# First stage of a two-block transformer kernel: token scale moved into the band matrix, Pool products ordered by token tile, one stacked one-hot product

## The reference

```
def rmsnorm(x, g):
    y = xf * lax.rsqrt(jnp.mean(xf * xf, axis=-1, keepdims=True) + EPS)
    return (y * g.astype(jnp.float32)).astype(x.dtype)

def pool_mixer(h, w, scale):            # h = rmsnorm(x, norm_mixer[0]), T = 256, D = 1024
    for g, win in enumerate((2, 4, 8, 16)):        # four groups of 256 features
        window_sum = csum[:, 1:, sl] - jnp.take(csum[:, :, sl], start, axis=1)
        outs.append(window_sum / cnt[None, :, None] - hf[:, :, sl])
    d = jnp.stack(outs, axis=2).astype(h.dtype)
    y = jnp.einsum('btgc,gce->btge', d, w).reshape(B, T, D)
    return y * scale

x = x + pool_mixer(rmsnorm(x, norm_mixer[0]), pool_w[0], pool_scale[0])
x = x + swiglu(rmsnorm(x, norm_ffn[0]), w_gate_up[0], w_down[0])
```

## Time and profile before

| what | value |
|---|---|
| median of 3 runs | 1152.99 us (1152.88 to 1153.0) |
| the profiled execution's own time | 1156.47 us |
| its span | 1154.5 us |
| PE busy | 1130.8 us, 98% of the span |
| DVE, ACT busy | 778.4 us (67%), 536.0 us (46%) |
| DMA | 204.57 MB, mean 177 GB/s |

### The profile page before, as it was taken

One profiled execution on the slowest core, in us unless ns is written; L12 is line 12 of the kernel. 1 busy time (PEld: TensorE's weight loads), 2 busy tenths in 40 slices (PEclk: granted clock), 3 DMA queues, 4 the chain that ended last, 5 costly groups with the idle time before them and its releaser, 6 DMA issues. The chain is left out here.

```text
span 1154.5 us, 16968 instructions
## 1 busy us (share of the span) xinstructions
PE 1130.8 (98%) x6628; PEld 983.2 (85%) x6628; DVE 778.4 (67%) x998; ACT 536.0 (46%) x704; POOL 32.8 (3%) x47
## 2 busy tenths in 40 slices
PE   6999999999999999999999999999999999999997
PEld 6788888898888888879988888888899888888886
DVE  4866666856667666677576676666766766766665
ACT  4633333466654334444566443334446655343332
POOL 0000000000000000003000000000030000000000
PEclk9999999999999999999999999999999999999999
DMA  8665555673356555668423465556673234656550
GB/s 271 224 201 183 200 182 189 222 245 113 118 174 230 187 182 182 207 153 264 144 104 103 148 230 195 182 182 201 179 235 110 75 111 145 219 188 201 181 193 37
DMA packets 167131, 204.57 MB, mean 177 GB/s; under 512 B 19988, under 2 KB 150028, under 8 KB 167078
## 3 DMA queue, kind: packets, MB, share of 16 engines
q1 hardware_dynamic: 167078, 203.84, 55.1%
HBM read 202.66 MB, written 1.16 MB: 177 GB/s over the span
## 5 line engine op out<-in xcount | busy, mean ns | idle before, releaser
L633 ACT ACTIVATE whi<-raw 128x2048 fp32r<-128x2048 f32 x176 | 336.4, 1914 | 381.2 <-PE bank L1514 247.2
L948 DVE TENSOR_TENSOR wlo<-raw,whi 128x2048 fp32r<-128x2048 f32 x171 | 392.0, 2294 | 163.1 <-ACT whi L633 163.0
L1510 PE MATMUL bank<-h_both,whi 128*128 128x512 f32 x1280 | 304.6, 390 | 0.0
L1510 PEld LDWEIGHTS bank<-h_both,whi 128*128 128x128 f32 x1280 | 237.7, 188 | 47.7
L1484 PE MATMUL bank<-whi,o_hi 128*128 128x512 f32 x448 | 176.2, 393 | 0.0
L1485 PE MATMUL bank<-wlo,o_hi 128*128 128x512 f32 x448 | 174.9, 390 | 0.0
L1486 PE MATMUL bank<-whi,o_lo 128*128 128x512 f32 x448 | 174.4, 389 | 0.0
L1514 PEld LDWEIGHTS bank<-h_both,wlo 128*128 128x128 f32 x1280 | 164.1, 191 | 6.2
L1514 PE MATMUL bank<-h_both,wlo 128*128 128x256 f32 x1280 | 166.0, 283 | 0.0
L1486 PEld LDWEIGHTS bank<-whi,o_lo 128*128 128x128 f32 x448 | 84.1, 188 | 18.0
L1484 PEld LDWEIGHTS bank<-whi,o_hi 128*128 128x128 f32 x448 | 84.3, 188 | 17.7 <-issue 1.3
(11 more groups left out here) (176 smaller groups left out, 1181.0 us busy)
## 6 DMA issues: line engine op xcount, KB each, us to landing
raw<-in_w_gate_up SPq DMA_DIRECT2D x44, 1024.0 KB, 5.1
raw<-in_w_down SPq DMA_DIRECT2D x44, 1024.0 KB, 4.9
raw<-in_w_gate SPq DMA_DIRECT2D x22, 1024.0 KB, 5.3
raw<-in_w_up SPq DMA_DIRECT2D x22, 1024.0 KB, 5.3
raw<-in_w_in SPq DMA_DIRECT2D x20, 1024.0 KB, 5.9
raw<-in_w_o SPq DMA_DIRECT2D x12, 1024.0 KB, 5.0
raw<-in_w_kv SPq DMA_DIRECT2D x8, 1024.0 KB, 5.4
raw<-in_w_q SPq DMA_DIRECT2D x4, 1024.0 KB, 5.4
```

The costliest lines, as they stand in the source:

```text
L633: act.activation(whi[:, s, :], raw[:, s, :], ACT.Copy).then_inc(hi_ready, 1)
L948: dve.tensor_tensor(wlo[:, s, :], raw[:, s, :], whi[:, s, :].bitcast(F32), ALU.subtract).then_inc(lo_ready, 1)
L1510: pe.matmul(bank[bk + jj][:, :], hi[:, kc, jj * P:(jj + 1) * P], h_both[:, kc, :, :].rearrange("p a t -> p (a t)"), start=(kc == 0), stop= ...
```

## The change

- The gain is no longer replicated over all partitions: its 1024 numbers are loaded as 8 rows of 128, PE transposes them to 8 columns (L1659), ACT copies these to `gcol` (L763). They are applied as a per-partition scale when d is copied out of the banks: ACT and DVE now do so in 8 pieces of 256 columns each (L777, L1298), DVE with a `scalar_tensor_tensor`.
- x itself is the stationary operand of the band products. The token scale `rstd` goes into the band: one `tensor_scalar` of 128x640 for each token tile (`scaled_band`, L1274) in place of four `normalise` of 128x512. The band is stored once (160 instead of 272 columns for each group), partition-major.
- The fourth square goes to DVE (`tensor_tensor_reduce`, L1278).
- ACT and DVE split both halves of the Pool weights ahead of all copies of d.
- The Pool products run in the order (0,0), (0,1), (1,0), (1,1), into banks 4 to 7; `first_norm` is rewritten for that order.
- The two tables and the two one-hot matrices are stacked at partitions 0 and 64: one product (L1690, 97 rows, 24 columns of weights), one copy (L678). Their loads stand ahead of the first gate weights on SP, behind a wait for three memsets on DVE. The product waits for the third `pool_scale`, since it uses bank 6.
- The identity matrix is loaded as the third DMA.

```
-            load_gain(0)
-            sp.dma_start(band, c["c_band"].rearrange("g p n -> p g n")).then_inc(band_in, 16)
+            sp.dma_start(ident[:, :], c["c_ident"]).then_inc(ident_in, 16)
+            sp.dma_start(gain_rows, GAIN_SRC[0].rearrange("(k p) -> k p", p=P)).then_inc(gains_in[0], 16)
+            sp.dma_start(band, c["c_band"].rearrange("p g n -> p (g n)")).then_inc(band_in, 16)
...
+            sp.wait_ge(ones_set, 2)
+            sp.dma_start(tables[0:NBUCKET, 0:16], a["rel_bias"]).then_inc(table_in, 16)
+            sp.dma_start(tables[T5_ROW:T5_ROW + NBUCKET, 16:24], a["t5_table_2"]).then_inc(table_in, 16)
+            sp.dma_start(onehots, c["c_onehots"]).then_inc(onehot_in, 16)
             load(k8(ffn_weights(0)[0], 0), FFN_U[0])
-            sp.dma_start(ident[:, :], c["c_ident"]).then_inc(ident_in, 16)
...
-            for t in range(TT):
-                for h in range(2):
-                    square(0, t, h)
+            for t, h in ((0, 0), (0, 1), (1, 0)):
+                square(0, t, h, 2 if t else 1)
+            act.wait_ge(gain_turned, 1)
+            act.activation(gcol[:, :], bank[7][:, 0:KC], ACT.Copy).then_inc(gcol_ready, 1)
...
+            for part in range(2):
+                pool_whi(part)
+            act.wait_ge(gcol_ready, 1)
             for k in range(4):
-                if k % 2 == 0:
-                    pool_whi(k // 2)
                 act.wait_ge(pool_d, k + 1)
-                act.activation(h_hi[:, 2 * k:2 * k + 2, :], bank[k][:, :].rearrange("p (c k) -> p c k", c=2),
-                               ACT.Copy).then_inc(hT_hi, 1)
+                for c_ in (2 * k, 2 * k + 1):
+                    i = act.activation(h_hi[:, c_, :], bank[k][:, (c_ % 2) * T:(c_ % 2 + 1) * T], ACT.Copy, scale=gcol[:, c_:c_ + 1])
+                i.then_inc(hT_hi, 1)
...
                     pool_scale(0, 0)
-                    pool_scale(1, 0)
                     pool_add(0, 0)
                     pool_scale(0, 1)
                     pool_add(0, 1)
-                    pool_scale(1, 1)
+                    pool_scale(1, 0)
                     mean_square(1, 0)
                     normalise(1, 0, 0)
                     normalise(1, 0, 1)
                     pool_add(1, 0)
+                    pool_scale(1, 1)
+                    h_lo_out(1, 0, 0)
                     pool_add(1, 1)
-                    h_lo_out(1, 0, 0)
                     h_lo_out(1, 0, 1)
...
+            def scaled_band(t):
+
+                if t == 0:
+                    dve.wait_ge(band_in, 16)
+                dve.wait_ge(rstd_ready, t + 1)
+                dve.tensor_scalar(band_s[t], band, rstd[:, t:t + 1], None, ALU.mult).then_inc(xn_ready, 2)
 
             mean_square(0, 0)
-            normalise(0, 0, 0)
+            dve.wait_ge(x_in[1], 16)
+            dve.tensor_tensor_reduce(xn[:, 1, HALF:], x[:, 1, HALF:], x[:, 1, HALF:], 1.0 / D, 0.0, ALU.mult, ALU.add,
+                                     ssq[:, 1, 1:2]).then_inc(last_square, 1)
+            scaled_band(0)
+            dve.wait_ge(last_square, 1)
             mean_square(0, 1)
-            normalise(0, 0, 1)
-            for h in range(2):
-                normalise(0, 1, h)
+            scaled_band(1)
...
-            for h in range(2):
-                pe.wait_ge((pool_lo, lo_ready)[h], 1)
-                for t in range(TT):
+            for t in range(TT):
+                for h in range(2):
+                    pe.wait_ge((pool_lo, lo_ready)[h], 1)
...
+            pe.wait_ge(pool_out, 3)
+            pe.matmul(bank[6][0:24, :], tables[:, :], onehots, start=True, stop=True).then_inc(vec_done, 1)
```

More of the change, by code:

```diff
@@ L51 @@
 IN_W = 2720
-BAND_W = 2 * P + 16
+BAND_W = P + 32
+T5_ROW = 64
 POOL_U = 0
@@ L86, in shape_constants @@
     t = np.arange(T)
-    band = np.zeros((4, P, BAND_W), f)
+    band = np.zeros((P, 4, BAND_W), f)
     for g, win in enumerate((2, 4, 8, 16)):
@@ L234, in bass_two_stacks @@
         wukv = sb("wukv", [P, 4, 2, HD])
-        band = qall[:, :, :].rearrange("p k t -> p (k t)")[:, 0:4 * BAND_W].rearrange("p (g n) -> p g n", g=4)
-        onehots = bias[:, 0:2 * SEQ_D].rearrange("p (i n) -> p i n", i=2)
-        vecs = bias[:, 2 * SEQ_D:4 * SEQ_D].rearrange("p (i n) -> p i n", i=2)
+        band_flat = qall[:, :, :].rearrange("p k t -> p (k t)")
+        band = band_flat[:, 0:4 * BAND_W]
+        band_s = [band_flat[:, (1 + i) * 4 * BAND_W:(2 + i) * 4 * BAND_W] for i in range(TT)]
+        gain_rows = xn[0:KC, 0, 0:P]
+        onehots = bias[0:T5_ROW + NBUCKET + 1, 0:SEQ_D]
+        vecs = bias[:, SEQ_D:2 * SEQ_D]
         pool_y = pr[:, 0:4, :, :].rearrange("p i a b -> p i (a b)")
@@ L633, in split, with square @@
                     act.activation(whi[:, s, :], raw[:, s, :], ACT.Copy).then_inc(hi_ready, 1)
-            def square(version, t, h):
+            def square(version, t, h, count=1):
                 if version:
@@ L644, in square @@
                 act.activation(junk[:, :], x[:, t, h * HALF:(h + 1) * HALF], ACT.Square, scale=1.0 / 32,
-                               accum_out=ssq[:, t, h:h + 1]).then_inc(squares, 1)
+                               accum_out=ssq[:, t, h:h + 1]).then_inc(squares, count)
             def h_out(j, t, h):
@@ L1276, in pool_wlo @@
                                   ALU.subtract).then_inc((pool_lo, lo_ready)[part], 1)
+            for part in range(2):
+                pool_wlo(part)
+            dve.wait_ge(gcol_ready, 1)
             for k in range(4):
-                if k % 2 == 0:
-                    pool_wlo(k // 2)
                 dve.wait_ge(hT_hi, k + 1)
-                dve.tensor_tensor(h_lo[:, 2 * k:2 * k + 2, :], bank[k][:, :].rearrange("p (c k) -> p c k", c=2),
-                                  h_hi[:, 2 * k:2 * k + 2, :].bitcast(F32), ALU.subtract).then_inc(hT_lo, 1)
+                for c_ in (2 * k, 2 * k + 1):
+                    i = dve.scalar_tensor_tensor(out=h_lo[:, c_, :], in0=bank[k][:, (c_ % 2) * T:(c_ % 2 + 1) * T],
+                                                 scalar=gcol[:, c_:c_ + 1], in1=h_hi[:, c_, :].bitcast(F32),
+                                                 op0=ALU.mult, op1=ALU.subtract)
+                i.then_inc(hT_lo, 1)
             ffn(0)
@@ L1664, in _ @@
             used(mm)
-            pe.wait_ge(ones_set, 3)
+            pe.wait_ge(ones_set, 2)
             pe.wait_ge(table_in, 32)
-            pe.wait_ge(onehot_in, 32)
-            K = NBUCKET + 1
-            for i, lhs in enumerate((tab_moba[0:K, :], tab_t5[0:K, :])):
-                pe.matmul(bank[6 + i][0:lhs.shape[1], :], lhs, onehots[0:K, i, :], start=True, stop=True).then_inc(vec_done, 1)
+            pe.wait_ge(onehot_in, 16)
+            pe.wait_ge(pool_out, 3)
+            pe.matmul(bank[6][0:24, :], tables[:, :], onehots, start=True, stop=True).then_inc(vec_done, 1)
             def ffn(f):
```

63 lines of the change are left out of this document (29 added, 34 removed).

## The result

| | median (range, executions) |
|---|---|
| before | 1152.99 us (1151.73 to 1157.84, 20) |
| changed | 1154.76 us (1153.97 to 1155.65, 20) |

The account below looks back on a forecast made before the run. PE's work plus its idling bounds the kernel, early on via a DVE chain to tile 1's transposes. 1.8 + 1.42 - 0.1 - 0.65 = 2.5 us off 1152.99 gives 1150.5 us, range 1149.0 to 1152.7.

Parts of the forecast that it names:

- At nothing: Parts forecast to change no time: single one-hot product (saves about 0.9 us of PE, hidden), tables' loads, one ACT copy less.
- The tables' loads: they finish long before: Table and one-hot loads moved ahead of the gate weights: claimed to finish long before needed, so worth nothing.
- first band product earlier: Kernel start: band lands at 7.8, its scale takes 0.55, so PE starts at 8.4 instead of 10.20, 1.8 us earlier.
- from there to the first Pool product: Band products keep shapes and count, so still 10.6 us, from 8.4 to 19.0; no gain.
- new order, up to `normalise` of tile 0: Pool products: `normalise` needs two chunks, not three; 12 matmuls less save 1.42 us, minus 0.1 for DVE.
- scale (1,1) in DVE's chain: Between tile 0's `normalise` and tile 1's transposes: one more 128x512 DVE operation gives back 0.65 us.
- The power: POOL's power for tile 0's rstd, slowed beside DVE's square, ends at 7.6, before the band lands at 7.8.
- The one-hot product: Single product before tile 0's transposes: ends at 26.7 while xn comes at 27.1, so its saving is worth nothing.
- the copies in eight pieces: Copies of d after the band products: last low part at 21.0, wanted at 22.8, so hidden with 1.8 to spare.
- Rival 2: Clock rises early, at the second tile's band products: 3.7 us more, gain 6.2, 1146.8 us; chance 0.11.
- rival 4: Clock stays low through the first gate passes, which end 2.2 us later than before: 1155.3 us; chance 0.04.
- Rival 3: Front doesn't move, small transfers costing what the saved bytes gain: PE starts at 10.2, gain 0.7, 1152.3 us; chance 0.13.

Follow-up runs that it names:

- 128-row kernel: Changed kernel with the one-hot matrices stored and loaded as 128 rows instead of 97, the product still reading 97: 1150.62 us, ratio 0.9988 to before.
- 96 idle rows: Kernel before plus a load of 96 rows that nothing reads, ahead of the first gate weights: 1152.94 us, ratio 0.9999.
- 97 rows late: Changed kernel, 97-row one-hots kept, with tables and one-hots loaded in their old place behind the first up weights: 1154.99 us, ratio 1.0014 to before.
- second profile of before: Kernel before, unchanged, run and profiled again: 1152.62 us beside 1152.74, ratio 0.9999; profile span 1150.7 us.
- the square on ACT: Changed kernel with 128 stored one-hot rows and the fourth square back on ACT instead of DVE: 1150.37 us in one execution.
- two variants with the same front and order: Changed kernel with 128 one-hot rows: table and one-hot loads in their old place, 1150.47 us; or DVE's first-half up-weight split behind tile 1's `normalise`, 1150.69 us.
- 106 rows: Kernel before plus a load of 106 rows that nothing reads, ahead of the first gate weights: 1157.16 us, ratio 1.0039.
- 99 rows: Kernel before plus a load of 99 rows that nothing reads, ahead of the first gate weights: 1152.72 us, ratio 1.0.
- 97 idle rows: Kernel before plus a load of 97 rows that nothing reads, ahead of the first gate weights: 1161.05 us, ratio 1.0071.

## Why the prediction was wrong

**The step that failed** is, in "At nothing", "The tables' loads: they finish long before". I asked whether the moved loads are late for their own reader (they weren't: at 19.38 for a product at 22.88), and not what they do to the load behind them. The one-hots held one engine and with it 1/16 of the gate weights, which are waited for by ACT, behind which stand the squares. It cost 4.00 us at tile 1's transposes (33.97 against 29.97) and turned 2.1 us gained into 1.8 lost. The spans differ by more, 1153.5 against 1148.4: 1.2 us more is the fall of the clock at 523 us. The same matmuls are 3.97 us later in the changed kernel up to 522 us (the transposes just ahead: 521.24 and 517.27), and 5.20 us later from 528 us on. Where the 128-row kernel has sixteen matmuls 0.12 us apart, the changed one has them 0.21 apart:

```profile
523.08 0.42 PE L1558 MATMUL bank<-whi,h_both 128*128 128x256 f32 x1
523.30 0.42 PE L1559 MATMUL bank<-wlo,h_both 128*128 128x256 f32 x1
```

and the 128-row kernel:

```profile
519.02 0.28 PE L1559 MATMUL bank<-whi,h_both 128*128 128x256 f32 x1
519.14 0.28 PE L1560 MATMUL bank<-wlo,h_both 128*128 128x256 f32 x1
```

PE idled 1.35 us ahead of them, and 1.36 at the same place in the 128-row kernel, where nothing fell. Of the thirteen profiles of this case three more have a fall near there (522.3 us with 96 idle rows, 523.3 with 97, 516.6 with 97 rows late); why one falls and the other doesn't stays open. The fall at 28 us cost nothing: from `normalise` to the next transposes 7.17 us, against 7.15 at full clock, since DVE's chain sets that time.

**The other steps**, measured between the second profile of before and the 128-row kernel:

| term | predicted | measured |
|---|---|---|
| first band product earlier | 1.8 | 10.19 - 8.58 = 1.61 |
| from there to the first Pool product | 0 | 7.97 - 7.84 = 0.13 |
| new order, up to `normalise` of tile 0 | 1.42 - 0.1 = 1.32 | 7.75 - 6.40 = 1.35 |
| scale (1,1) in DVE's chain | -0.65 | 6.54 - 7.15 = -0.61 |
| sum | 2.5 | 2.48 |

Behind the first row: the band was there for its scale at 8.14 in the changed kernel, 7.97 with 128 rows and 7.81 with the square on ACT (forecast 7.8, bounds 7.2 and 8.3); the scale took 0.55 as estimated. The power ended at 7.4 (forecast 7.6) and is off the path: with the square on ACT it ended 0.5 earlier than in the 128-row kernel (6.69 against 7.20), and the chain from the band on was the same. The one-hot product, the gain's transpose and the copies in eight pieces were hidden as said.

**The clock.** Rival 2 had its place right: the rise falls among the second tile's band products, in the changed kernel and in each of its variants (the 48 products take 8.45 and 8.07 us in the two shown, 8.17 to 8.56 in the other five, where they took 11.01). In the trace its price is right too: 36.09 to 29.97 is 6.1 us, where I had worked out 6.2. But the kernel before gains by it as well: 36.09 to 32.45 in its two profiles, 3.6 us, where the rival had 3.7, and the execution with the early rise lies at the median (1152.76 beside 1152.62), the one with the late rise 3.5 above it. So it is no gain of the change. I had taken these 3.5 us as constant, and they weren't: the profiled execution lies 0.8 above the median in the changed kernel and 0.2 below it with 128 rows. That the forecast of 1150.5 fits the 128-row kernel all the same is in part luck: the sum compares two executions that both have the late clock, and so holds for two that both have the early one. Here the Trainium skill (TensorE: Matmul & The Clock Gate, "Part 1: The HAM clock gate") would have told more than the one trace: sustained matmul activity releases the clock; I had set it aside on a late rise in one execution. The traces agree: in the twelve other profiles the rise came 3.3 to 5.8 us after the first band product, in that one 12.8.

Two near hits are luck as well. The transposes of tile 1 came at 33.97, and I had forecast 33.6: the early clock had put the first Pool product at 16.96 instead of 19.0, and the late weights took it back. And 1154.76 is near the 1155.3 of rival 4 (its own sum gives 1155.2: 1152.99 + 2.2), but not by its mechanism: there the clock doesn't rise ahead of the first gate pass, here it rose at 14.26, fell at 27.9 behind PE's idle time, and was low for the first 2 us of that pass (from 29.26), at no cost. Rival 3 did not come about: PE started 1.45 us earlier in the changed kernel.

**A version that beats both** is the change with 128 stored rows: 1150.62 us. Its interval ends at 0.9999, just short of no difference from before, but two variants with the same front and order gave the same gain (0.9985 and 0.9984). Twelve executions of it reach up to 1154.59; which event makes the slowest three so is not in the profiled one, and stays open. Their distance from the median, 3.9 us, is near what the late clock cost the kernel before (3.6), but no profile shows it.

## What to carry to other kernels

For every load that is added or moved ahead of another, work out on how many engines its rows go (largest divisor of the rows up to 16) and what stands behind it on those engines; pad 97 rows to 128, as here. Ask of a moved load not only whether its own reader gets it in time, but who waits for the last share of the loads behind it. And where the profiled execution lies 3 us from the median, find out what differs before building a sum on its clock.

## What the runs showed of the hardware

- The number of landings on a load's semaphore follows the row count as if it told how many engines took part: 97 rows 2 landings, 106 rows 3, 99 rows 12, 96 and 128 rows 16. Where that makes fewer than 16 engines, one landing comes 0.45 to 0.60 us after the issue.
- 194 KB in 97 rows took 13.4 us from the first to the second landing; 256 KB in 128 rows were there at 13.22, issued at the same place of the queue.
- A GpSimd power of 0.55 us takes 0.93 beside DVE's square with two SBUF reads, and 0.55 without it.
- The length of an idle stretch of PE alone doesn't tell whether the clock falls: it fell to half within 6.01 us (the kernel before with 97 idle rows), and behind 3.69 us (the changed kernel, 0.50 granted from 28 to 31), 3.25 us (106 rows) and 1.62 us (96 rows, 0.50 from 28 to 30.5), but not behind 3.05 us (97 rows late, 1.00 granted from 20 to 30); and at 523 us behind 1.35 us in one kernel and not behind 1.36 us in another.
- A fall doesn't always cost time: the one at 523 us cost the changed kernel 1.2 us; the one at 28 us cost nothing, since PE was waiting for DVE's chain; and the kernel with 97 rows late, which has one at 516.6 us, is 3.3 us behind the 128-row kernel on both sides of it.
- Ahead of the first recorded rise the granted clock reads 1.00, though the matmuls go at half the pace: 8.75 to 14.00 us in the changed kernel, and 10.20 to 20.80.
